# Handing the attention block's output over to the even block in two halves of 256 tokens, with the scaling on GpSimd

## What is computed, cut to what matters here

```python
        # end of the attention block (first_block)
        mixed = (jax.nn.sigmoid(gate_a) * y_mla + jax.nn.sigmoid(gate_b) * y_fox) @ w_out[l]
        h = h + rmsnorm(mixed, post_norm_g[l])
    return h[:, N_META:]

    # start of the even block (second_block, layer 0)
        xn = rms_norm(h, norm_mix[layer])
        if layer % 2 == 0:
            proj = jnp.einsum('bsd,de->bse', xn, w_in_even[i])
            a_b = proj[..., 0:A_WIDTH]
            a_c = proj[..., A_WIDTH:2 * A_WIDTH]
            a_v = proj[..., 2 * A_WIDTH:3 * A_WIDTH]
            z_b = proj[..., 3 * A_WIDTH:]
            y_a = short_gated_conv(a_b, a_c, a_v, conv_a[i])
            y_b = multiscale_pool(z_b, w_pool[i], pool_scale[i])
            mix = jnp.concatenate([y_a, y_b], axis=-1)
            h = h + jnp.einsum('bse,ed->bsd', mix, w_out_even[i])
```

## Time and profile before

| | |
|---|---|
| time, median of 3 runs | 1788.53 us (1787.32 to 1789.47) |
| the profiled execution | 1785.2 us; span from first to last instruction 1783.5 us |
| busy share of the span | PE 96%, PEld 80%, DVE 53%, ACT 44%, POOL 23% |
| granted TensorE clock, mean | 0.994 |
| the whole stage of the change | about 720 to 812 us of the span |

### The profile page before, as it was taken

How to read it: one execution, slowest core, us unless ns; L and a number is a source line. 1 busy time by engine, 2 the same in 40 slices (tenths; PEclk the granted TensorE clock), 3 DMA queues, 4 the chain that set the end, 5 groups by cost and what they waited for, 6 DMA issues and landing times.

```text
span 1783.5 us, 25326 instructions
## 1 busy us (share of the span) xinstructions
PE 1719.1 (96%) x8460; PEld 1427.8 (80%) x8460; DVE 952.3 (53%) x1736; ACT 787.3 (44%) x1373; POOL 412.4 (23%) x555
## 2 busy tenths in 40 slices
PE   7899998999989999899999999999999999999998
PEld 6777877898978888578878888888888788888886
DVE  6677775776773334675455555433346555555332
ACT  6667766566662224333333333322363433333222
POOL 3546565555530001300211111011003211111000
PEclk9999999999999999899999999999999999999999
DMA  4112122333323334123333333333332233333332
GB/s 135 51 44 62 38 61 60 85 74 70 82 62 99 98 94 138 52 78 106 95 94 95 94 94 94 114 97 98 94 94 71 83 98 96 98 96 92 92 97 86
DMA packets 284312, 154.39 MB, mean 87 GB/s; under 512 B 12655, under 2 KB 278770, under 8 KB 284242
## 3 DMA queue, kind: packets, MB, share of 16 engines
q1 hardware_dynamic: 281858, 148.95, 29.1%
q0 software_dynamic: 2336, 4.47, 1.1%
q10 hardware_dynamic: 48, 0.07, 0.0%
HBM read 147.02 MB, written 2.16 MB: 84 GB/s over the span
## 4 chain that ended last, share of the span: by engine, by line
PE 82%; DVE 6%; ACT 4%; POOL 4%; issue 3%; DMA 0%; ACTq 0%; DVEq 0%; POOLq 0%
PE ps L361 67%; PE ps L970 5%; PE ps L2382 2%; POOL w_split L318 1%; PE ps L802 1%; PE ps L823 1%; PE ps L784 1%; ACT w_split L304 1%; POOL w_split L320 1%; DVE tmp L1298 1%; PE ps L673 1%; PE ps L836 1%; POOL arena_r L1455 1%; DVE arena_r L1334 1%; PE ps L810 1%
## 5 line engine op out<-in xcount | busy, mean ns | idle before, releaser
L361 PE MATMUL ps<-u,w_split 128*128 128x512 f32 x3825 | 911.0, 395 | 13.2 <-DVE u L1962 8.4
L361 PEld LDWEIGHTS ps<-u,w_split 128*128 128x128 f32 x3825 | 714.9, 189 | 176.8 <-DVE u L1962 8.7
L320 DVE TENSOR_TENSOR w_split<-w_raw,w_split 128x1024 fp32r<-128x1024 f32 (+1 forms) x221 | 268.2, 1213 | 434.2 <-ACT w_split L304 434.1
L304 ACT CAST w_split<-w_raw 128x1024 fp32r<-128x1024 f32 (+4 forms) x321 | 289.1, 915 | 416.1 <-PE ps L361 381.2
L361 PE MATMUL ps<-arena_r,w_split 128*128 128x512 f32 x1824 | 417.2, 390 | 1.7 <-DVE arena_r L2522 1.7
L361 PEld LDWEIGHTS ps<-arena_r,w_split 128*128 128x128 f32 x1824 | 341.9, 188 | 74.1 <-DVE arena_r L2522 3.3
L2302 POOL TENSOR_TENSOR tmp<-tmp 128x512 f32<-128x512 f32 x44 | 56.9, 1293 | 423.7 <-ACT tmp L2287 423.7
L318 POOL TENSOR_TENSOR w_split<-w_raw,w_split 128x256 fp32r<-128x256 f32 x168 | 122.2, 757 | 16.1 <-ACT w_split L304 15.4
L1811 POOL TENSOR_TENSOR tmp<-tmp 128x512 f32<-128x512 f32 x40 | 56.6, 1415 | 269.8 <-ACT tmp L1770 234.5
L970 PE MATMUL ps<-u,w_split 128*128 128x264 f32 x768 | 105.8, 287 | 2.4 <-POOL w_split L318 2.2
L970 PEld LDWEIGHTS ps<-u,w_split 128*128 128x128 f32 x768 | 98.6, 189 | 5.0 <-POOL w_split L318 2.7
(11 more groups left out here) (265 smaller groups left out, 1588.2 us busy)
## 6 DMA issues: line engine op xcount, KB each, us to landing
w_raw<-in_w_in_dram SPq DMA_DIRECT2D x118, 256.0 KB, 3.2
w_raw<-in_w_ffn_gate_dram SPq DMA_DIRECT2D x88, 256.0 KB, 3.1
w_raw<-in_w_ffn_up_dram SPq DMA_DIRECT2D x88, 256.0 KB, 3.1
w_raw<-in_w_ffn_down_dram SPq DMA_DIRECT2D x64, 256.0 KB, 3.0
w_raw<-in_w_in_even_dram SPq DMA_DIRECT2D x32, 256.0 KB, 3.1
w_raw<-in_w_in_odd_dram SPq DMA_DIRECT2D x32, 256.0 KB, 3.1
w_raw<-in_w_ffn_down_dram SPq DMA_DIRECT2D x32, 192.0 KB, 2.6
w_raw<-in_w_br_mla_dram SPq DMA_DIRECT2D x16, 256.0 KB, 3.0
```

Source lines behind the costliest of these rows:

```text
L304: ins = act.copy(dst, src)
L320: ins = eng.tensor_tensor(lo, r, hi, ALU.subtract)
L361: last = pe.matmul(out_ap, w_tile(c, ws, k - n0), moving(k, ms), start=start and n == 0, stop=stop and n == len(total) - 1, skip_group_che ...
```

## The change

The last two out tiles and the first two groups of the even block are made in two halves of 256 tokens (`side(0)`, `side(1)`), each in its own PSUM bank region. PE's order becomes: tile 6 half 0, tile 7 half 0, then half 1 of tile 6 with the sums and the spread of half 0 inside it, half 1 of tile 7, then groups 0 and 1 over half 0, with the sums and the spread of half 1 inside, then over half 1. `add`, high, `low` and squares are made by halves, all 8 tiles of half 0 and then all of half 1. Of the 16 scalings POOL makes 13 and DVE 3 (tile 0 half 0, tiles 6 and 7 half 1). The norm of the even block is no longer summed up on POOL tile by tile: the squares go into `m2`, POOL adds three pairs, and PE sums the 5 tiles that are left with 20 one-column matmuls. The splits of EZ and EZ+1 come later in DVE's list, after the first adds.

```diff
+        LAST_OUT = (KT - 2, KT - 1)
+        SIDE_BANKS = {(KT - 2, 0): 2, (KT - 1, 0): 3, (KT - 2, 1): 0, (KT - 1, 1): 1}
...
+            side_product(six, 0, range(KT)).then_inc(sem("side"), 1)
+            pe_x(pe, six)
...
+            side_product(seven, 0, range(KT)).then_inc(sem("side"), 1)
+            pe_x(pe, seven)
+            pe.wait_ge(sem("m2"), 6)
+            side_product(six, 1, range(3), stop=False)
+            pe_side_sums(pe, 0)
+            side_product(six, 1, range(3, KT - 1), start=False, stop=False)
+            pe_side_rbc(pe, 0)
+            side_product(six, 1, (KT - 1,), start=False).then_inc(sem("w_used"), 1)
+            side_product(seven, 1, range(KT)).then_inc(sem("w_used"), 1)
...
+            side_rms(0)
+            side_square(KT - 2, 1)
+            side_rbc(0)
+            w_hi(act, EZ)
+            high(0, 0)
+            high(1, 0)
+            side_square(KT - 1, 1)
+            w_hi(act, EZ + 1)
...
-        POOL_SCALED = (1, 3, 5)
+        BY_DVE = ((0, 0), (KT - 2, 1), (KT - 1, 1))
...
+        E_PAIRS = (0, 2, 4)
+
         def pool_out(pool):
-            pool.wait_ge(sem("m2"), KT)
-            pool.wait_ge(sem("out_rsb"), 1)
-            for n in POOL_SCALED:
-                pool.tensor_tensor(m2[:, n, :], m2[:, n, :], rbc[:, 0, :], ALU.mult).then_inc(sem("res_pool"), 1)
+            for n, g in pool_scaled():
+                if (n, g) == (1, 0):
+                    pool.wait_ge(sem("m2"), KT)
+                    pool.wait_ge(sem("out_rsb"), 1)
+                elif (n, g) == (0, 1):
+                    pool.wait_ge(sem("out_rsb"), 2)
+                pool.tensor_tensor(m2[:, n, side(g)], m2[:, n, side(g)], rbc[:, 0, side(g)], ALU.mult) \
+                    .then_inc(sem("res_pool"), 1)
+            for n in E_PAIRS:
+                pool.wait_ge(sem("squared"), tiles_before("e") + KT + n + 2)
+                pool.tensor_tensor(m2[:, n, :], m2[:, n, :], m2[:, n + 1, :], ALU.add).then_inc(sem("acc_done"), 1)
...
         def pe_even(pe):
...
+            w_ready(pe, EZ + 2)
+            pe.wait_ge(sem("res"), len(BY_DVE))
+            product(pe, bank(E_BANKS[2]), EZ + 2, u_real, range(3), stop=False)
+            pe.wait_ge(sem("squared"), tiles_before("eo"))
+            pe.wait_ge(sem("acc_done"), acc_before("eo"))
+            sources = [n for n in range(KT) if n - 1 not in E_PAIRS]
             for t in range(NQ):
-                ins = pe.matmul(bank(6, t, t + 1), acc[:, 0, t * P:(t + 1) * P], ones[:, 0:1], start=True, stop=True)
+                for n in sources:
+                    ins = pe.matmul(bank(6, t, t + 1), m2[:, n, t * P:(t + 1) * P], ones[:, 0:1],
+                                    start=n == 0, stop=n == KT - 1, skip_group_check=True)
             ins.then_inc(sem("summed"), 1)
+            product(pe, bank(E_BANKS[2]), EZ + 2, u_real, range(3, KT), start=False).then_inc(sem("w_used"), 1)
+            w_ready(pe, EZ + 3)
+            product(pe, bank(E_BANKS[3]), EZ + 3, u_real, range(2), stop=False)
+            pe.wait_ge(sem("diagonal"), 3)
             pe.matmul(bank(7), ones[:], sq[:, 0, :], start=True, stop=True).then_inc(sem("e_bc"), 1)
```

More of the change, by code:

```diff
@@ L1803, in pool_squares @@
         def pool_squares(pool, tag):
-            for n in range(KT - 1 if tag in ("out", "down1") else KT):
+            for n in range({"out": KT - 2, "down1": KT - 1}.get(tag, KT)):
                 pool.wait_ge(sem("squared"), tiles_before(tag) + n + 1)
@@ L1880, in pe_out @@
                     pe.wait_ge(sem("m2"), n - 3)
[L1881 to L1900, removed]
@@ L1901, in pe_out @@
-            pe.wait_ge(sem("diagonal"), 1)
-            pe.wait_ge(sem("h_x"), KT)
-            for b in (7, 5):
-                pe.matmul(bank(b), ones[:], sq[:, 0, :], start=True, stop=True).then_inc(sem("out_rbc"), 1)
+                product(pe, bank(n % 4), OUT + n, u_real,
+                        ready=(lambda k: pe.wait_ge(sem("mr_lo"), k + 1)) if n == 0 else None) \
+                    .then_inc(sem("w_used"), 1)
+                pe_x(pe, n)
+            six, seven = LAST_OUT
+            w_ready(pe, OUT + six)
@@ new lines, in side_rbc, with high, square @@
+            def side_rbc(g):
+                act.wait_ge(sem("out_rbc"), g + 1)
+                act.copy(rbc[:, 0, side(g)], bank(7 if g == 0 else 5, g * SIDE, (g + 1) * SIDE)) \
+                    .then_inc(sem("out_rsb"), 1)
+            def high(n, g):
+                act.wait_ge(sem("h_tile"), KT * g + n + 1)
+                act.activation(u_side(g)(n, HI), h[:, n, side(g)], ACT.Copy, scale=vcol("mix_g", n)) \
+                    .then_inc(sem("hs_hi"), 1)
+            def square(n, g):
+                act.activation(m2[:, n, side(g)], h[:, n, side(g)], ACT.Square).then_inc(sem("squared"), 1)
@@ L1909, in act_out @@
+            for n in range(KT - 2):
                 act.wait_ge(sem("w_used"), OUT + n + 1)
@@ L1934, in dve_out @@
+            side_rbc(1)
+            for n in (5, 6, 7):
+                square(n - 5, 0)
+                high(n, 0)
+            for n in range(KT):
+                high(n, 1)
+                if n < KT - 3:
+                    square(n + 3, 0)
+                else:
+                    square(n - KT + 3, 1)
+            for n in range(3, KT):
+                square(n, 1)
+        BY_DVE = ((0, 0), (KT - 2, 1), (KT - 1, 1))
         def dve_out(dve):
             mixed_lo(dve, (KT - 1,))
-            for n in range(KT):
+            for n in range(KT - 2):
@@ new lines, in dve_out @@
+            dve.wait_ge(sem("h_x"), KT)
+            dve.wait_ge(sem("out_rsb"), 1)
+            scale(0, 0)
+            add(0, 0)
+            add(1, 0)
+            w_lo(dve, EZ)
+            low(0, 0)
+            add(2, 0)
+            low(1, 0)
+            add(3, 0)
+            low(2, 0)
+            dve_side_diagonal(dve, 1)
+            w_lo(dve, EZ + 1)
+            add(4, 0)
+            low(3, 0)
+            for n in range(5, KT):
+                add(n, 0)
+                low(n - 1, 0)
@@ L2035, in pe_even @@
-            w_ready(pe, EZ + 3)
-            product(pe, bank(3), EZ + 3, u_real).then_inc(sem("w_used"), 1)
+            product(pe, bank(E_BANKS[3]), EZ + 3, u_real, range(2, KT), start=False).then_inc(sem("w_used"), 1)
             for g in range(GROUPS):
```

230 lines of the change are left out of this document (143 added, 87 removed).

## The result

The changed kernel takes 1793.42 us, median of nine runs (1792.0 to 1796.64), beside 1789.47 us of the kernel before on the same chip (nine runs, 1787.32 to 1793.22). The ratio is 1.0023, with a 95% interval of 1.0014 to 1.0032: slower by about 4 us. The forecast was 1792.8 us, 4.3 us slower.

The account below looks back on a forecast made before the run. The prediction took DVE, with ACT and POOL around it, to bound the hand-over and PE's rate the rest. EC+3's +2.5 us and the clock's +1.8 gave +4.3 on the 1788.5 median: 1792.8 us, range 1787.0 to 1797.0.

Parts of the forecast that it names:

- Start of DVE's stretch: In the hand-over, DVE's first scaling starts at 732.85 us against 737.28, earlier by 4.4 us.
- Length of it: DVE's hand-over stretch takes 25.8 us against 23.5: 16.5 own work, 9.3 POOL turns; last `low` ends at 758.7.
- the third case: In the hand-over, DVE and POOL at half width disturb each other little; 1784.8 us, chance 0.09.
- To EZ+2: After the last `low`, three matmuls and a split: EZ+2 starts at 761.7 us instead of 764.29, earlier by 2.6.
- What it gives back: In EZ+2, 20 sums cost 3.9 us and the spread ends 5.2 us later; EC+3 starts 2.5 us late.
- the fifth case: In EZ+2, sums of five tiles take one record each, 2 us in all, without a clock fall; 1789.0 us, chance 0.08.
- The clock after the sums: Behind the 20 sums in EZ+2, the clock falls to 1.2 GHz and the next nine matmuls cost 1.8 us more.
- The second case: In EZ+2, the clock holds through the 20 sums; 1791.0 us, chance 0.23.
- The clock in the sparse stretch: Before 761 us, where PE works less than half the time, the clock is down as well: 1.2 us more.
- the fourth case: In the hand-over, half-wide instructions have more fixed cost, or the clock falls before 761 us; 1796 us, chance 0.20.
- EC and EC+3: First and fourth conv units wait for DVE's splits: EC starts 2.1 us late, EC+3 2.5 us late, before the clock term.
- Sum: Whole kernel: +2.5 and +1.8 give +4.3 us, put on the median 1788.5 for 1792.8 us.

Follow-up runs that it names:

- e7: Changed kernel with all 16 scalings on DVE and each `low` one tile later; 1791.14 us, ratio 1.0005 to the kernel before.
- e3: Changed kernel with all 16 scalings on DVE, none on POOL, in the order as it stands; 1798.68 us, ratio 1.0047 to the kernel before.
- e5: Changed kernel with the norm's spread 9 matmuls behind the 20 sums instead of 21; 1793.43 us, ratio 1.0016 to the kernel before.
- e8: e7 with the early spread of e5 added; 1789.50 us, ratio 0.9996 to the kernel before.
- e4: Changed kernel with 16 filler matmuls into an unused bank in PE's sparse stretch; 1792.42 us, ratio 1.0015 to the kernel before.
- e2: Changed kernel with the 20 sums cut into four blocks of 5, 3 matmuls of EZ+2 between blocks; 1794.41 us, ratio 1.0022 to the kernel before.
- e1: Changed kernel with 4 one-column sums in place of 20, the other tiles left out of the norm; 1788.27 us, ratio 0.9984 to the kernel before.
- e10: e9 with EC's split also placed ahead of the norm's spread; 1787.69 us, ratio 0.9981 to the kernel before.
- e6: Changed kernel with POOL summing all eight tiles' squares, 4 sums behind EZ+2's product; 1792.82 us, ratio 1.0012 to the kernel before.
- e9: e7 with e6's POOL tree, EZ+3's split ahead of the square root, 4 sums three matmuls into EZ+3; 1789.73 us, ratio 0.9996 to the kernel before.

## Why the prediction was right, and where it was not

The time was right within 0.6 us of the median, and the direction right. By its own steps:

- **Start of DVE's stretch.** Forecast 732.85, in the trace 732.73.
- **Length of it.** Forecast 25.8 us and an end at 758.7; it took 25.1 and ended at 757.85. Half-wide `add` and `low` take 0.94 to 0.95 us beside POOL and 0.47 to 0.48 alone, start to start 0.87 and 0.40; 0.40 was the charge for one alone. The Trainium skill's rule on the two engines (SBUF — State Buffer, "Who interferes with whom") agrees with these numbers, and the third case, in which they disturb each other little, is out. e7 gives the price itself: 0.48 us a scaling where 0.6 was taken.
- **To EZ+2.** Forecast 761.7, in the trace 761.4.
- **What it gives back.** The 20 sums came in 40 records, as forecast, so the fifth case is out. They took 6.17 us instead of 3.9. This is the term that failed: the price was that of sums at 2.4 GHz, and the forecast let the clock fall behind them; it falls inside them, and the second half ran at 1.2 GHz. In e3, e5, e7 and e8, where the fall came later, they took 4.36 to 4.60, in e4 4.84. In the short run from which the forecast took its price, the fall stands at 46.7 us and not at 46.2 (0.83 over 46 to 47), behind the sums and the first full matmuls; no row of before has a fall inside a row of sums.
- **The clock after the sums.** Forecast +1.8 for the matmuls behind; they took 6.35 us for 21, 1.5 more than 4.84. The second case, in which the clock holds, is out. The step was right in kind and near in size.
- **The clock in the sparse stretch.** It stood in the fourth case, with 1.2 us, and not in the sum. It happened too: nine matmuls of EZ+2 took 3.3 us instead of 2.1, and e4 took this away and gave 1.0 to 1.4 us back. The section on DVE's stretch says that the clock there costs nothing since DVE is late anyway; that holds up to the last `low`, but the low clock outlasts it by nearly 6 us.
- **EC and EC+3.** The split ended 5.2 us after the spread by the forecast, 4.9 in the trace; PE waited there for 0.83 us, forecast 1.0. EC+3's 0.4 us more show only as 0.6 us in the 144 matmuls (33.78 us against 33.2 at 0.2305). Together EC started at 783.10 where 778.6 + 1.8 = 780.4 was forecast: 3.3 us more by the clock (sums 2.3, sparse stretch 1.3, behind the sums -0.3), less 0.6 by the earlier stretch and DVE's shorter list.
- **Sum.** In the traces the shift was 7.1 us and not 4.3. By the medians it was 4, so the agreement of the time is in part luck: the forecast's steps give a sum that is 2.8 us short of the trace, and it holds nothing that would bring the medians 3 us closer together than the traces. It took the 3.3 us by which the profiled execution of before lies under its median as noise that adds to both sides alike. For the kernel before the fourteen traces bear this out: tile 6 can start 5 us later, and the part behind the stage can take 2.7 us more. The changed kernel's first trace has as early a start and yet lies at its own median. Shorter stretches of low clock in its runs without a trace, like those of e5 and e8, would explain this; that is not shown.

## What to carry to other kernels

Where a hand-over is bound by one engine, look at what the shorter hand-over leaves in the path behind it before counting the gain: here VectorE was done 2.9 us earlier, the norm's spread still ended 9.9 us later, and the fixes that paid were fewer tiny matmuls, the waiting engine's splits placed ahead of the norm, and the scalings kept on VectorE in an order that gives ScalarE one tile's time. Work moved from VectorE to GpSimd isn't simply taken off when both read SBUF: measure what it costs the first (here 0.48 us for 0.33 us of work). And before a sum from one trace is put on a median, compare stages that the change doesn't touch over several traces: here their lengths differed by as much as the whole effect.

## What the runs showed of the hardware

The clock fell at a row of one-column matmuls though the records show PE as busy all the time: in all eight traces with 20 sums (the changed kernel twice, e2, e3, e4, e5, e7 and e8) the clock fell to 1.2 GHz within or right behind them. Of the four with 4 sums, e1 and e10 show no fall behind them, and e6 and e9 one each, behind an idle time of 2.5 and 2.9 us. It stayed low for 6.8 us in the changed kernel, e2 and e4, and for 3.4 us in e3, e5, e7 and e8. The rows at 768 to 772 us of the changed kernel, 2.00 of 2.00 us busy at 0.50, show it best. The Trainium skill (TensorE: Matmul & The Clock Gate, "What's actually happening") has the clock follow how busy the engine has been; taken by the busy time of the records, these rows don't fit it. Spreading the sums between full matmuls (e2) did not help.

The turns of VectorE and GpSimd also reach a weight split: EZ+2's low part takes 1.23 us alone and 1.53 beside a GpSimd addition (e7), and in e10 two splits in a row took 3.77 us beside GpSimd's additions instead of about 2.4 (1.14 and 1.23 alone).
